# The recurrent layer's norm, input products, convolution, gates, scans and GELU as one written-out stage without GpSimd, its GELU branch last

## The reference, cut to what matters

```python
def second_block(x, ...):
    # layer 0: windowed attention, then an expert layer
    x = layer_norm(ALPHA * x + mix, ln_mix_g[0], ln_mix_b[0])
    ffn = expert_choice_moe(x, ...)
    x = layer_norm(ALPHA * x + ffn, ln_ffn_g[0], ln_ffn_b[0])   # "the norm" below
    # layer 1
    mix = bidir_rglru_block(x, ...)
    ...

def bidir_rglru_block(x, w_in, conv_w, conv_b, w_rgate, b_rgate, w_igate, b_igate, lam, w_out):
    gate_br, xb = jnp.split(x @ w_in, 2, axis=-1)          # x: 1024 tokens x 1024; w_in: 1024 x 2048
    xp = jnp.pad(xb, ((0, 0), (2, 1), (0, 0)))
    xc = conv_b
    for j in range(4):
        xc = xc + conv_w[j] * xp[:, j:j + S]
    xr = xc.reshape(B, S, 4, 256)                          # the gates are block diagonal: 4 blocks of 256
    r = sigmoid(einsum(xr, w_rgate) + b_rgate)             # for 2 directions
    i = sigmoid(einsum(xr, w_igate) + b_igate)
    log_a = -8 * r * softplus(-lam)
    a = exp(log_a)
    mult = sqrt(-expm1(2 * log_a))                         # 1 at each direction's first token
    u = mult * i * xc
    h = scan(a[0], u[0]) + scan(a[1], u[1], reverse=True)  # h[t] = a[t] * h[t-1] + u[t]
    return (h * gelu(gate_br)) @ w_out
```

## Time and profile before

| what | value |
|---|---|
| median of 3 runs | 5081.05 us |
| the profiled execution, its own time | 5079.31 us |
| its span | 5077.5 us |
| PE busy | 4260.5 us (84%) |
| DVE busy | 1593.9 us (31%) |
| ACT busy | 1081.3 us (21%) |
| POOL busy | 374.3 us (7%) |
| mean granted PE clock | 0.921 |

### The profile page before, as it was taken

How to read it: one execution, slowest core, us unless ns; L and a number is a source line. 1 busy time by engine, 2 the same in 40 slices (tenths; PEclk the granted TensorE clock), 3 DMA queues, 4 the chain that set the end, 5 groups by cost and what they waited for, 6 DMA issues and landing times. The chain is left out here.

```text
span 5077.5 us, 63957 instructions
## 1 busy us (share of the span) xinstructions
PE 4260.5 (84%) x23058; PEld 2197.5 (43%) x23059; DVE 1593.9 (31%) x2847; ACT 1081.3 (21%) x1779; POOL 374.3 (7%) x353
## 2 busy tenths in 40 slices
PE   7899987888977759948898599999498656999996
PEld 4555436774433324424454344444243223444442
DVE  3354554442211122231283611110233647011112
ACT  1154224441100101110163100000212632000001
POOL 0000002320000020010000000000000410000000
PEclk8899999999988879979899799999699877999998
DMA  2131244422213169961004488888411023888885
GB/s 87 66 125 41 62 171 98 89 54 80 83 50 119 59 241 361 362 251 65 21 1 154 153 304 308 307 312 312 140 33 29 21 112 130 280 314 306 308 309 179
DMA packets 428166, 824.81 MB, mean 162 GB/s; under 512 B 146768, under 2 KB 288208, under 8 KB 394960
## 3 DMA queue, kind: packets, MB, share of 16 engines
q1 hardware_dynamic: 399696, 722.73, 41.2%
q0 software_dynamic: 17216, 60.83, 4.1%
q10 hardware_dynamic: 11072, 38.67, 1.9%
HBM read 696.28 MB, written 125.86 MB: 162 GB/s over the span
## 5 line engine op out<-in xcount | busy, mean ns | idle before, releaser
L2825 PE MATMUL ec1e_pg<-ec_wg,ec1e_xT 128*128 128x512 f32 x1024 | 444.3, 594 | 2.2 <-DVE ec1e_xT L2878 2.2
L2825 PE MATMUL ec0e_pg<-ec_wg,ec0e_xT 128*128 128x512 f32 x1024 | 443.6, 594 | 2.1 <-DVE ec0e_xT L2878 2.1
L2825 PEld LDWEIGHTS ec1e_pg<-ec_wg,ec1e_xT 128*128 128x128 f32 x1024 | 195.3, 191 | 248.3 <-issue 248.3
L2825 PEld LDWEIGHTS ec0e_pg<-ec_wg,ec0e_xT 128*128 128x128 f32 x1024 | 195.1, 191 | 247.7 <-issue 247.7
L1371 PE MATMUL mix_pb<-h_h_all,mix_wg 128*128 128x512 f32 x512 | 222.8, 595 | 12.2 <-DMA mix_wg<-in_w_in_dram 12.2
L1861 PE MATMUL exp_pg<-exp_wb,exp_xT 128*128 128x512 f32 x512 | 224.6, 597 | 6.3 <-DMA exp_wb<-in_w_dram 6.3
L2851 PE MATMUL ec1e_py<-ec_wd,ec1e_hidT 128*128 128x512 f32 x512 | 223.4, 594 | 0.0
L2851 PE MATMUL ec0e_py<-ec_wd,ec0e_hidT 128*128 128x512 f32 x512 | 223.4, 594 | 0.0
L679 PE MATMUL front_pz<-h_h_all,front_w 128*128 128x512 f32 x480 | 211.7, 599 | 8.7 <-DMA front_ones<-in_head_ones_dram 8.7
L2186 PE MATMUL gqap_pq<-gqap_w,gqap_xT 128*128 128x512 f32 x384 | 180.7, 631 | 21.5 <-DVE gqap_xT L2231 17.6
L3159 PE MATMUL lrus_pw<-lruk_xc,lrus_w 128*128 x256 | 119.5, 629 | 60.7 <-ACT lrus_r L3193 46.8
(11 more groups left out here) (541 smaller groups left out, 6325.2 us busy)
## 6 DMA issues: line engine op xcount, KB each, us to landing
ec_wg<-in_moe_w_gate_up_dram SPq DMA_DIRECT2D x256, 1024.0 KB, 6.6
ec_wd<-in_moe_w_down_dram SPq DMA_DIRECT2D x256, 512.0 KB, 4.5
exp_wb<-in_w_dram SPq DMA_DIRECT2D x64, 1024.0 KB, 13.8
exp_w2b<-in_w_dram SPq DMA_DIRECT2D x32, 1024.0 KB, 14.1
wkv_inp<-arrays SPq DMA_DIRECT2D x160, 128.0 KB, 3.0
arrays<-front_out SPq DMA_DIRECT2D x36, 512.0 KB, 5.7
yb<-mlaa_zero SPq DMA_DIRECT2D x1, 16384.0 KB, 52.3
yb<-exp_y ACTq DMA_DIRECT2D x32, 512.0 KB, 6.5
```

Of the source, the lines that this page charges most:

```text
L2825: return nc.tensor.matmul(pg[:, b, :], xT[:, k, :], wg[:, k, b * HALF:(b + 1) * HALF], start=k == 0, stop=k == KD - 1)
```

## The change

Phases "ec0n", "lrui" and "lrus" become one phase, `lru_mix`, with every loop unrolled; the attention layer's `layer_tail` no longer ends with a norm.

- **Norm.** The normalised tile `o` is transposed from SBUF as soon as it is made; it is also stored to DRAM, where "ec1p" reads it. The norm's two vectors `gb` are loaded at the phase's start by ACT's DMA queue (before: inside the expert phase), with `ident` and `vec`. ACT copies each transposed tile between its norm steps.
- **PE's order.** First transposes of 4 tiles, then half products mixed with the other transposes, then for u = 0 to 7 a product of 16 matmuls and the 16 gate matmuls of tile u, then the remaining 6 products of the GELU branch. The products that feed the convolution come first; those of the GELU branch are last.
- **PSUM.** `pA` has 4 banks for the input products (2 tiles in turn), `pB` 4 banks, for transposes and then for the gates of one unit. A unit n is one channel tile in one direction (n = 2u + z); units share 3 sets of buffers.
- **ACT** applies the sigmoids by halves of 512 columns, right out of PSUM, and takes a^2 as exp(2 log a) (`dec[:, 1]` is -16 softplus). DVE takes POOL's product. POOL has no work in the phase.
- **GELU** is worked on halves of 512 columns: ACT squares from PSUM, DVE forms the cubic and `gh` = h times the branch, ACT the sigmoid, DVE the last product.
- **`xc` and `wd`** share one buffer: `w_out` is loaded into it within the phase, once the last gate product and DVE's last use of `xc` are done. The attention layer's `w_out` is loaded by the same helper in front of its `layer_tail` (its 4 DMAs now stand ahead of the two tiles `xt`, not among them).

```diff
-        with Phase(nc, "lruk") as kept:
-            ...
-            with Phase(nc, "lrui") as one:
-                lru_in(nc, one, vec, xc, vecs, w_in, eye, ident, x_dram, ggT)
-            with Phase(nc, "lrus") as two:
-                lru_scan(nc, two, vec, xc, w_r, w_i, ggT)
-        layer_tail(nc, "ec1", ggT, ident, *tail)
+        wd = ph.sb("wd", [P, KD, D])
+        wo_in = [ph.sem(f"wo_in{h}") for h in range(2)]
+        with Phase(nc, "lrui") as one:
+            lru_mix(nc, one, vecs, w_in, w_r, w_i, eye, ident, ln_ffn, acc_dram, x_dram, ggT, wd, w_out, wo_in)
+        layer_tail(nc, "ec1", ggT, ident, wd, wo_in, *tail)
...
+def lru_mix(nc, ph, vecs, w_in, w_r, w_i, eye, ident, ln_ffn, acc_dram, x_dram, ggT, xc, w_out, wo_in):
+    W_RING, SLOT = 3, 3
...
+        def _(sp):
...
+            for i in range(2, 5):
+                load_g(i)
+            sp.wait_ge(r_psum, 8 * KD)
+            sp.wait_ge(in_ready, 2 * KD)
+            load_w_out(sp, xc, w_out, wo_in)
+            for i in range(5, KD):
+                load_g(i)
...
+        def _(pe):
+            pe.wait_ge(consts, 64)
...
+            def gates(u):
+                pe.wait_ge(conv_done, u // 2 * 2 + 2)
+                pe.wait_ge(gw_ready[u % 2], 64 * (u // 2 + 1))
+                for z in range(2):
+                    n = 2 * u + z
+                    for k in range(2):
+                        for h in range(2):
+                            at = 2 * k + h
+                            if n:
+                                pe.wait_ge(r_kept, 4 * (n - 1) + at + 1)
...
+            for t in range(4):
+                turn(t)
+            branch(0, 0)
+            turn(4)
+            turn(5)
+            branch(1, 0)
+            turn(6)
+            turn(7)
+            branch(0, 1)
+            branch(1, 1)
+            for u in range(KD):
+                if u + 2 < KD:
+                    branch(u + 2, 0)
+                    branch(u + 2, 1)
+                else:
+                    gelu_in(u + 2 - KD)
+                gates(u)
+            for i in range(2, KD):
+                gelu_in(i)
...
+        def _(act):
...
+            for u in range(KD):
+                sigmoids(2 * u)
+                sigmoids(2 * u + 1)
...
+                decays(2 * u)
+                decays(2 * u + 1)
+                mults(2 * u)
+                mults(2 * u + 1)
+                if u + 3 > KD - 1:
+                    gelu(u + 3 - KD)
+            for i in range(3, KD):
+                gelu(i)
...
+        def _(dve):
...
+            def chain(u):
+                inputs(2 * u)
+                inputs(2 * u + 1)
+                minus_mult2(2 * u)
+                minus_mult2(2 * u + 1)
+                scan(2 * u)
+                scan(2 * u + 1)
+            def cubes(i, h):
+                at = 2 * (i % 2) + h
+                dve.wait_ge(squared, 2 * i + h + 1)
+                V.link(nc.vector.tensor_scalar(g2[:, h, :], g2[:, h, :], 0.044715, 1.0, ALU.mult, ALU.add))
+                nc.vector.tensor_tensor(g3[:, h, :], g2[:, h, :], pA[:, at, :], ALU.mult).then_inc(cube, 1)
+                nc.vector.tensor_tensor(gh[:, h, :], ggT[:, i, halves[h]], pA[:, at, :], ALU.mult).then_inc(g_free, 1)
...
+            for i in range(3):
+                conv(i)
+            for u in range(KD):
+                chain(u)
+                if u + 3 < KD:
+                    conv(u + 3)
+                else:
+                    gelu(u + 3 - KD)
+            for i in range(3, KD):
+                gelu(i)
```

More of the change, by code:

```diff
@@ L2102, in gqa_phase @@
                 gqa_attend(nc, two, sink, masks, ident, qT, kT, v, oT)
-        layer_tail(nc, "ec0", oT, ident, *tail)
+        with Phase(nc, "gqaw") as last:
+            wd = last.sb("wd", [P, KD, D])
+            wo_in = [last.sem(f"wo_in{h}") for h in range(2)]
+            load_w_out(nc.sync, wd, w_out, wo_in)
+            layer_tail(nc, "ec0", oT, ident, wd, wo_in, *tail)
 def gqa_project(nc, ph, w_qkv, eye, rope, x_dram, ident, qT, kT, v):
@@ new lines, in turn, with product @@
+            def turn(t):
+                pe.wait_ge(o_ready, t + 1)
+                if t >= 2:
+                    pe.wait_ge(xT_ready, t - 1)
+                for k in range(KD):
+                    m = nc.tensor.transpose(pB[:, 2 * (t % 2) + k // 4, k % 4 * P:(k % 4 + 1) * P], o[t % 4][:, k * P:(k + 1) * P], ident[:, :])
+                m.then_inc(x_psum, 1)
+            def product(q, bank, h):
+                pe.wait_ge(w_ready[q % W_RING], 16 * (q // W_RING + 1))
+                pe.wait_ge(xT_ready, 4 * h + 4)
+                for k in range(KD):
+                    m = nc.tensor.matmul(pA[:, bank, :], w[:, q % W_RING, k, :], xT[:, k, halves[h]], start=k == 0, stop=k == KD - 1)
+                return m
@@ new lines, in sigmoids @@
+            def sigmoids(n):
+                u, z = n // 2, n % 2
+                r, ig, _, _ = unit(n)
+                if n >= SLOT:
+                    act.wait_ge(h_ready, n - SLOT + 1)
+                elif n == 2:
+                    for v in range(4):
+                        act.wait_ge(o_out[v], 16 * (NT // 4))
+                for k, (dst, b0) in enumerate(((r, br), (ig, bi))):
+                    for h in range(2):
+                        act.wait_ge(r_psum, 4 * n + 2 * k + h + 1)
+                        at = b0 + z * KD + u
+                        nc.scalar.activation(dst[:, halves[h]], pB[:, 2 * k + h, :], ACT.Sigmoid, bias=vec[:, at:at + 1]).then_inc(r_kept, 1)
@@ L3181, in _ @@
+            sums(0)
+            for t in range(NT):
+                if t + 1 < NT:
+                    sums(t + 1)
+                squares(t)
+                if t:
+                    roots(t - 1)
+                if t >= 2:
+                    keep_x(t - 2)
+            roots(NT - 1)
+            keep_x(NT - 2)
+            keep_x(NT - 1)
+            act.wait_ge(consts, 64)
             nc.scalar.activation(sm[:, 0, :], vec[:, lam:lam + 2 * KD], ACT.Abs).then_inc(sp_a, 1)
```

486 lines of the change are left out of this document (240 added, 246 removed).

## The result

The changed kernel takes 4951.52 us, the median of 4 runs (4939.51 to 4954.70), against 5079.60 before, the median of 4 (5074.20 to 5082.69): ratio 0.9745, 95% interval 0.9733 to 0.9756. The forecast was 4949.

The account below looks back on a forecast made before the run. The stretch was taken as bound by dependence, not by an engine. From t0, 65.0 + 302.1 + 9.4 + 2 + 4.5 + 1.2 = 384.2 us put "ec1p" 131.5 earlier, so 4949 us was predicted, range 4932 to 4985.

Parts of the forecast that it names:

- the front: Norm, transposes and half products at the phase's start: 32 matmuls done 65.0 us after the norm's first tile load.
- the GELU waits: At tiles 5 and 6, PE waits for ACT's GELU sigmoids and DVE's cubic: 4.7 us twice, 9.4.
- the clock behind them: PE's clock may fall after the two GELU waits: 2 us taken, 5.2 by the skill page's rule.
- the end: After PE's last matmul: 4.5 us of last GELU half plus 1.2 for phase end and start; `w_out` landed long before.
- Where t0 lies: Load of the norm's first tile, t0: three phase ends now ahead of it add 1.5 us (0 to 2.5), giving 3613.3.
- DVE's last normalised tile ... holds nobody: In the norm, DVE's last normalised tile is ready by 45.4 us and delays no other engine.
- cold start of the first half product: PE's first 8 matmuls after the norm's first transposes: 6.9 us plus a cold start of 2.6.
- The gate loop: The remaining 352 matmuls cost only PE's own time, 302.1 us, if PE never waits for ACT or DVE.
- Rival A: Gate loop: a GELU-like wait and cold start in the other six tiles, 41 us, 4990; 0.15 shared with the clock rival.
- C: PE's clock falls to 0.90 in the dense matmuls, losing 40 us, 4989; 0.15 shared with the every-tile-wait rival.
- Rival B: Next tile's gates can't begin before the last one's scans and taps end: 230 us of stall, 5180; chance 0.03.
- Rival D: More hides: vectors land with the first tile, no cold start, no GELU wait; 18 us less, 4931; chance 0.04.

Follow-up runs that it names:

- e9: The changed kernel unchanged, second profile: 4949.34 us; stage (load of the norm's first tile to first product of "ec1p") 390.1.
- e1: Changed kernel, but SP loads the norm's two vectors ahead of the tiles and DVE no longer waits for `vec`: 4948.84 us, stage 389.1.
- e2: Changed kernel, but SP issues one weight tile, then the norm's stores with the other weight loads between them: 4950.63 us, stage 384.9.
- e8: Changed kernel with three edits: norm's vectors first, stores before later weights, GELU's sigmoids between the gate sigmoids: 4936.76 us, ratio 0.9716 to the kernel before, stage 371.9.
- e7: Changed kernel, but units take turns in two sets of buffers instead of three: 4951.78 us, stage 387.4.
- e5: Changed kernel, but all convolution input products come first, then the gates, not interleaved: 5001.67 us, ratio 0.9844 to the kernel before, stage 438.1.
- e3: Changed kernel, but ACT takes GELU sigmoids 0 and 1 between the next tile's gate sigmoids: 4939.82 us, ratio 0.9723 to the kernel before, stage 377.0.
- e6: Changed kernel, but POOL again makes the product of input gate and `xc`: 4954.45 us, stage 390.1.
- e4: Changed kernel, but `w_out` is loaded after the phase's end, not prefetched: 4956.04 us, ratio 0.9752 to the kernel before, stage 392.0.
- e10: The changed kernel unchanged, third profile: 4948.38 us, stage 384.15.

## Why the prediction was right

The total was right to 2.5 us, and the stage (384.2 against 384.1 in the profile) more closely than its terms were. That closeness is luck: the front was 4.8 us longer than forecast, the matmuls of the loop took 0.7 more, and the GELU waits, the clock behind them and the end together 5.5 less; in e9, the same kernel, the stage is 390.1. The mechanism, and the size of the largest term, were right.

- **Where t0 lies.** Forecast 3613.3. The three profiles of the changed kernel have 3605.3, 3609.8 and 3613.95. The first is 12 us under the kernel's median of 4951.5 in own time, in good part for this reason: it was early long before the changed stage, with the first product of the attention layer's `layer_tail` at 2692.19, against 2694.37 and 2699.04 in the other two. The shift of 1.5 for the three phase ends comes out smaller: from PE's last product of the expert phase to t0 it is 12.8 us before (3598.95 to 3611.75) and 13.4 to 13.7 in the three profiles, so 0.6 to 0.9.
- **The front was mis-sized, 69.8 instead of 65.0.** The vectors landed as forecast, at 8.1 against 8. What was missed is that DVE's first step waits for `ident` and `vec` too, by one semaphore, and `vec` landed at 11.7: DVE started there and not at 8.5. That alone would not have counted, as e1 shows. The step that counts is "DVE's last normalised tile ... holds nobody": it counted DVE and ACT, not the store that frees a buffer nor the loads ahead of that store on SP. That cost 3.98 us on DVE. e2 shows it by moving the store; e1, that the vectors alone are worth nothing while it stands; e8, that both together bring the first half product 5.9 us forward from t0, 5.0 from SP's first load. Against that, the cold start of the first half product was 8.49 - 7.03 = 1.5 here, not 2.6 (up to 3.1, in e7). The first full product began at 56.0 instead of 51.3.
- **The gate loop, 302.1 if PE never waits: right.** No wait in the first five tiles, clock 1.00. Rival A (a wait in every tile) and C (a falling clock) did not occur. e5 shows how near A was without the products in between: 6.87 us a tile.
- **The GELU waits, 9.4 forecast, 6.5 measured.** (The forecast's own times, 39.0 - 34.4, give 4.6 a wait, not 4.7.) Their place, count and releaser were right, the size was not. The chain on DVE came out as forecast (the first cubic done 34.8 us after its tile's gates began, against 35.4). The table load was placed behind the wait for it, as the earlier trace rows had suggested; it stands ahead and hides in 5.25 us of waiting. That is 1.3 of the 1.5 us a wait. e3 removes both waits and 7.1 us of the stage.
- **The clock after them, 2 with bounds 0 and 5.2.** Both ends are real: 0 in two profiles of the changed kernel and 5.8 in the third, the upper end a little passed. The value of 2 describes none of the three; among the variants e7 comes near it, with 1.7. The rule in the HAM oscillation section of the Trainium skill's TensorE: Matmul & The Clock Gate page, that bursts behind waits start cold, is borne out by both waits of e1, e2, e5, e6 and e9, by one of e7's two, and by neither in e4, e10 and the first profile, at waits of one length. The Trainium skill's ScalarE: Activation LUTs page, in its section on rules for kernel authors, budgets 2.7 us a switch, which would have made the two waits longer; they came out shorter, and the trace has 1283 ns a load.
- **The end, 5.7 forecast, 5.1 measured.** Its `w_out` part is confirmed by e4: 8 us. The attention layer's `w_out`, forecast 0 with bounds of 1, has PE waiting for it 9.67 us instead of 9.42 (9.55 in e9 and e10).
- **Rival B, the serial chain,** rested on the three unit buffers. e7 has two, and PE still does not wait. It is refuted with room to spare.
- **Rival D's mechanism** was real in part: at GELU more hid than was forecast.

Of what POOL did, the product is worth nothing on PE's path (e6, 384.1 left). Its square of `a`, beside which the backward scans took 5.62 us, was not put back alone, nor were the unrolling, the halved sigmoids or a^2 on ACT undone.

Of the 133.1 us, 62 are shown by taking the part out again: the interleaving (54.0, e5) and the early load of `w_out` (8, e4); the first was undone with all other edits in place, so part of it may be theirs too. The other 71 are read from the traces and not tried: the 9.5 left of the loop, the 27.7 of the front, where the norm's tiles no longer go to DRAM and back ahead of the first transpose, and the 33.8 left of the end, where 82.4 us of PE's GELU products now run beside the last chains that PE waited for before.

## What to carry to other kernels

Between two chains bound by dependence, look first for independent matmuls to set among them: 16 input matmuls a tile hid all of ACT's and DVE's chain. When a phase is joined with its neighbour, walk each queue in issue order: a store that frees a buffer stood behind eleven loads that nobody needed yet. Compare variants by one stage of the trace and by the bursts in it; here 6 us of clock would have hidden a gain of 3.6 and shown a loss where there was none. And where an edit moves a load ahead of the point from which you count, count from that load.

## What was not expected of the hardware

- At a wait of 3.24 us the granted clock falls in one execution and not in another: of 18 such waits in nine profiles (changed, e1, e2, e4 to e7, e9, e10), 11 were followed by 8 matmuls in 8.5 to 10.2 us and 7 by 7.13. e5's waits of 6.87 us were followed by a slow burst every time (5 of 5). The waits of 1.24 us ahead of the row of 27.70 never were.
- Three loads of 512 KB behind 4 MB of tiles held SP's issue for 12.38 us (12.34 in both repeats), where a gate weight's load takes 0.47. In e2 the first one alone took 0.50. What in them holds the queue, their form or what is in flight, stays open.
- The forward and backward scans cost the same, 2292 and 2291 ns, where POOL is idle. Before, what was stretched was the operation that began second: a backward scan 0.16 us behind the start of POOL's square took 5.62 us, while a scan that began 0.42 us ahead of POOL's product took 2.27, the product 6.18 instead of 4.52, and DVE's sum of the two scans, which began during the product, 5.27 instead of 1.23. In e6 the product ran beside DVE's taps, which read one of their tiles from PSUM, and neither was stretched.
